# Prompt attention: query tiles in descending order, and the bias strip loaded by head

## What is computed

```python
def attend(q, k, v, bias, mask):
    s = jnp.einsum('bntkgd,bnlkd->bnkgtl', q, k).astype(F32) * HEAD_DIM ** -0.5 + bias
    m = mask[:, None, None]
    p = jax.nn.softmax(jnp.where(m, s, NEG_INF), axis=-1)
    p = jnp.where(m, p, 0.0)
    o = jnp.einsum('bnkgtl,bnlkd->bntkgd', p.astype(v.dtype), v)
    return o, p
...
    g = jax.nn.sigmoid(gate_logit.astype(F32)).reshape(B, T, NSA_KV_HEADS, NSA_GROUP, 3).astype(o_cmp.dtype)
    o = g[..., 0:1] * o_cmp + g[..., 1:2] * o_sel + g[..., 2:3] * o_win
```

## Time and profile before

| what | value |
|---|---|
| median of 3 runs | 1068.53 us (1065.99 to 1071.66) |
| the profiled execution | 1066.85 us |
| its span, first to last instruction | 1064.9 us |
| TensorE busy | 959.9 us, 90% of the span |
| VectorE busy | 450.3 us, 42% |
| ScalarE busy | 310.9 us, 29% |
| GpSimd busy | 268.8 us, 25% |
| mean granted TensorE clock | 0.938 of full speed |

### The profile page before, as it was taken

How to read it: one execution, slowest core, us unless ns; L and a number is a source line. 1 busy time by engine, 2 the same in 40 slices (tenths; PEclk the granted TensorE clock), 3 DMA queues, 4 the chain that set the end, 5 groups by cost and what they waited for, 6 DMA issues and landing times. The chain is left out here.

```text
span 1064.9 us, 21167 instructions
## 1 busy us (share of the span) xinstructions
PE 959.9 (90%) x8113; PEld 632.8 (59%) x8113; DVE 450.3 (42%) x933; ACT 310.9 (29%) x712; POOL 268.8 (25%) x397
## 2 busy tenths in 40 slices
PE   6899999999899989998899998996599999999755
PEld 5456777777666858887455664454455555555422
DVE  2240000003667257785568772437522233333216
ACT  4100000000575213233367642101023232333222
POOL 6000000032102146900256523000223333444110
PEclk9899999999999989999899998997599998899888
DMA  9975642522920030000744252926599999999954
GB/s 309 343 284 215 214 178 100 107 85 75 320 69 7 1 48 3 4 4 7 186 116 119 71 188 107 335 98 256 224 356 381 386 394 380 391 369 366 366 192 146
DMA packets 89227, 207.76 MB, mean 195 GB/s; under 512 B 31526, under 2 KB 54750, under 8 KB 75231
## 3 DMA queue, kind: packets, MB, share of 16 engines
q1 hardware_dynamic: 76226, 182.64, 49.3%
q0 software_dynamic: 10144, 20.47, 6.0%
q10 hardware_dynamic: 2756, 3.27, 0.9%
HBM read 254.83 MB, written 29.75 MB: 267 GB/s over the span
## 5 line engine op out<-in xcount | busy, mean ns | idle before, releaser
L2403 POOL DMA_INDIRECT ys_dram<-late,ids x49 | 45.3, 924 | 155.4 <-ACT late L2605 129.4
L592 PE MATMUL PS<-hT,wring 128*128 128x288 f32 x256 | 83.5, 408 | 0.0
L2787 DVE COPY mixT<-PS 128x128 f32<-128x128 f32 x49 | 14.3, 292 | 163.0 <-PE PS L2513 163.0
L593 PE MATMUL PS<-hT,wring 128*128 128x288 f32 x256 | 83.0, 406 | 0.0
L2397 POOL DMA_INDIRECT mixT<-h_dram,ids x49 | 46.9, 957 | 110.2 <-DVE ids L2754 91.6
L2494 PE MATMUL PS<-ring,mixT 128*64 128x256 f32 x304 | 72.4, 393 | 2.4 <-DVE mixT L2773 2.4
L2495 PE MATMUL PS<-ring,mixT 128*64 128x256 f32 x304 | 72.4, 393 | 0.0
L2494 PEld LDWEIGHTS PS<-ring,mixT 128*64 128x64 f32 x304 | 43.1, 143 | 33.9 <-issue 12.6
L2427 PE MATMUL PS<-late,mixT 128*128 128x512 f32 x128 | 57.7, 611 | 1.8 <-PEq L2854 1.8
L592 PEld LDWEIGHTS PS<-hT,wring 128*128 128x128 f32 x256 | 48.2, 190 | 17.2 <-DVE xc L203 2.6
L593 PEld LDWEIGHTS PS<-hT,wring 128*128 128x128 f32 x256 | 48.6, 190 | 13.4
(11 more groups left out here) (566 smaller groups left out, 2206.0 us busy)
## 6 DMA issues: line engine op xcount, KB each, us to landing
ring<-in_expert_w_gate_dram SPq DMA_DIRECT2D x27, 1024.0 KB
ring<-in_expert_w_up_dram SPq DMA_DIRECT2D x27, 1024.0 KB
ring<-in_expert_w_down_dram SPq DMA_DIRECT2D x27, 1024.0 KB
late<-in_w_ada_dram SPq DMA_DIRECT2D x8, 2048.0 KB
mod_r<-in_expert_w_gate_dram SPq DMA_DIRECT2D x9, 1024.0 KB
mod_r<-in_expert_w_up_dram SPq DMA_DIRECT2D x9, 1024.0 KB
mod_r<-in_expert_w_down_dram SPq DMA_DIRECT2D x9, 1024.0 KB
late<-in_expert_w_gate_dram SPq DMA_DIRECT2D x7, 1024.0 KB
```

Source lines behind the costliest of these rows:

```text
L592: MM(PS[:, b, 0:HALF], lhs, hT[:, k, 0:HALF], **s)
L593: last = MM(PS[:, b + 1, 0:HALF], lhs, hT[:, k, HALF:NTOK], **s)
L2403: pool.indirect_dma_start(m.ys_dram.ap(), bass.IndirectOffsetOnAxis(ap=ids[:, 1, j:j + 1], axis=0), yr(n), None, bounds_check=LAST_ROW, oo ...
```

## The change

Three things are changed together. The prompt's query tiles are taken in descending order, so that the first units have 512 keys and the last 128. The bias strip is loaded by four transfers, one for each g, with the heads g and G + g and all 896 columns, in place of five transfers of all heads and a part of the columns. The waits of VectorE follow: once for each g in the first tile, in place of one for each tile and one for the first compressed unit. `out_of`, which picks the output bank and orders the outputs, counts in the new order.

```diff
-    strip_in = [sem(f"a_strip_in{k}") for k in range(5)]
+    strip_in = [sem(f"a_strip_in{g}") for g in range(G)]
...
-    for i in range(PT):
+    for i in reversed(range(PT)):
         units += [("p", SEL, i, g) for g in range(G)] + [("c", CMP, i, 0)] + [("p", WIN, i, g) for g in range(G)]
...
-    out_of = lambda u: units[u][2] + (PT if units[u][0] == "s" else 0)
+    out_of = lambda u: PT + units[u][2] if units[u][0] == "s" else PT - 1 - units[u][2]
...
-            for k, (lo, hi) in enumerate(((SEQ - P, SEQ), (SEQ, STRIP), (SEQ - 2 * P, SEQ - P), (P, 2 * P), (0, P))):
-                sp.dma_start(strip[:, :, lo:hi], bass.AP(m.rb_rep, RB_C - (SEQ - P) + lo, [[H * RB_W - 1, P], [RB_W, H], [1, hi - lo]])).then_inc(strip_in[k], 16)
+            for g in range(G):
+                sp.dma_start(strip[:, g::G, :], bass.AP(m.rb_rep, g * RB_W + RB_C - (SEQ - P), [[H * RB_W - 1, P], [G * RB_W, KV], [1, STRIP]])).then_inc(strip_in[g], 16)
...
                 if kind == "p":
-                    if br == SEL and g == 0:
-                        dve.wait_ge(strip_in[a if a == 0 else a + 1], 16)
+                    if br == SEL and a == PT - 1:
+                        dve.wait_ge(strip_in[g], 16)
...
                 elif kind == "c":
-                    if a == 0:
-                        dve.wait_ge(strip_in[1], 16)
...
                 if kind == "p":
-                    if a == 0 and g == 0:
+                    if a == PT - 1 and g == 0:
                         pe.wait_ge(pt_v if br == SEL else pt_a, 1)
```

## The result

Over 20 runs of each, the changed kernel has a median of 1071.88 us (1066.88 to 1076.64), the kernel before 1068.22 us (1060.23 to 1072.42): ratio 1.0037, 95% interval 1.0019 to 1.0055. The forecast was 1072 us, 0.3% above the 1068.53 us of the runs shown then.

What follows compares the result with a forecast made beforehand. Attention is paced in turn by a VectorE-ScalarE loop and by TensorE. Loads 1.1, order 3.6, sample head minus 2.4 and front clock 1.7 sum to plus 4.0 us: 1072 forecast, range 1065 to 1079.

Steps and rivals of the forecast that it cites:

- Start: First attention unit waits for 0.393 MB more of the bias strip: plus 1.1 us.
- The later strips: Bias loads after the first come 2.5 us apart, units want them at least 2.87 apart: hidden, no cost.
- Width changes: Prompt tiles in descending order, wide turning and values beside narrower scores: 90.3 against 86.75 us, plus 3.6.
- Tile 3: First prompt tile now: four units at 2.87, five at 3.11, 27.0 us against 24.6 without outputs and key copies, plus 2.4.
- Tile 0: Last prompt tile now: 15.92 less 3.0 of low clock, plus 1.72, 2.6 and 0.5, giving 17.7 us.
- The kernel before at full clock: Front of attention, tile 0 in the old order: the low clock loses 3.0 us.
- Head of the samples: First sample group after the prompt tiles falls from 10.71 to 8.3 us with one-block units left over: minus 2.4.
- Clock at the front: Start of attention: clock falls again, somewhat later, for 3.4 us at half rate, a lag of 1.7 us.
- Rival 1: Clock stays low at the front ten us or more under 512-key units: 5 in place of 1.7, 1076; chance 0.18.
- Rival 2: Clock falls under tile 0 at the prompt's end, the 3.0 us only change place: 1075.5; chance 0.10.
- Rival 3: Wide turns and values behind narrower scores are absorbed, tiles 2 and 1 lose their 3.7: 1069; chance 0.20.
- Rival 4: Strips land together, first unit waits for 3.67 MB, some 7 us go: 1079; chance 0.07.

Runs made afterwards that it cites:

- the second pair of profiles: The changed kernel and the kernel before, each profiled again with no code change; attention 143.00 us and 139.52 us.
- thinner values: Changed kernel with added front matmuls, two of four key blocks left out of tile 3's window value products; tile 2 22.82 us in place of 25.41.
- the order alone: Kernel before with query tiles descending, strip still loaded by columns; attention 151.26 us, total ratio 1.0127 (1.0058 to 1.0196).

## Why the prediction was right

The total, 1072, the sign and the size of attention's part (plus 4.0 forecast; plus 3.7 and, from the second pair of profiles, 3.5 measured) came out; several terms were off and made up for one another. That the total came out to 0.1 us is luck: the same code against itself was 0.5% off.

- Start: 1.1 forecast, 0.7 measured (4.74 against 4.06); the second pair's 0.6 is not the strip's, as both waited for TensorE. The queue moved 430 GB/s in the microsecond from 521, more than either rate I had. The Trainium skill, page "DMA: Bandwidth & Descriptors", section Specifications, puts the HBM limit of a core near 358 GB/s and asks for no more than 512 B a transfer for line rate. Here runs of 512 and 1,536 bytes went at 290 to 372 GB/s and runs of 3,584 bytes at 398 to 430 in the microseconds from 519 to 526, so the measurement decides for this case. The Trainium skill, page "Perfetto Trace Analysis", section Roofline, allows a core that works alone some 435 GB/s, and with that the trace agrees. The later strips were hidden, as forecast.
- Width changes. At full clock tiles 3, 2, 1, 0 take 25.74, 25.40, 20.66, 18.41 (forecast 27.0, 25.0, 20.6, 17.7), 90.22 together (90.3). Tile 2 and 1 were right to 0.4 and 0.1, and the cause, backlog on TensorE, was shown for tile 2 by thinner values. Tile 3 was over-priced by 1.3: its first four units took 11.0 us (11.5 forecast) and the five behind 14.7 (15.6), as only three of these stand 3.1 us apart; the step behind the compressed unit is 2.58 and the last 2.87. Tile 0 was under-priced by 0.7, and the next term explains it: from 13.80 us, the kernel before at full clock, the forecast's own additions (1.72, 2.6 and 0.5) give 18.6, 0.2 above the 18.41 measured. The key copies cost 2.7 there, so their price was right, TensorE's wait of 2.38 us at step 34 included.
- The kernel before at full clock: I took 3.0 us off tile 0, the run with added matmuls took off 2.1. The 3.0 came from the spacing of two units (1.97 against 1.43) for the whole low stretch.
- Head of the samples: minus 2.4 forecast, minus 3.7 measured, and 0.4 more in the second group, which I hadn't priced.
- Clock at the front: a fall was forecast between 526 and 530 and came at 529.7; it lasted 6.8 us in place of 3.4, cost 2.3 in place of 1.7, and showed as the idle of 2.27 us at the first window unit. Rival 1, ten us or more, came true in the second profile for the length (10.2 us), not the price: tile 3 took 28.32, 2.6 more than at full clock, where I had 5. In the first profile TensorE's second turning waits 1.53 us for a copy of ScalarE, in this one not at all, so part of the slow work filled waits that were there anyway. In the order alone 13.2 us of low clock under tile 3, from its start on, cost 1.3 (27.05). The place of the stretch counts for more than its length.
- Rival 2, a fall under tile 0, I had set beside the forecast; it came together with the front's, in most profiles, and costs 1.5 us (19.97 and 19.92 against 18.41).
- Rival 3 fell: nothing was absorbed, in any order. Rival 4 fell with the first score operation at 4.74 us; the order alone, which waits for all four pieces, stands at 13.70.

The account, at full clock: the order adds 5.7 us to the prompt (90.22 against 84.56) and takes 3.7 and 0.4 from the samples: plus 1.5. The clock costs the changed kernel 2.3 and 1.5, the one before 2.1: plus 1.7. The loads: plus 0.7. Sum 3.9, measured 3.7; the stage's last part, behind the start of the last sample group, was 0.15 shorter.

## What to carry to other kernels

In a software pipeline whose later steps work on earlier, wider units, a falling order makes narrow steps pay for wide ones where the engine of the later steps is near the limit, and gives part of it back behind the loop; here 5.7 us against 4.1. A rising order does the reverse. Choose loads to fit the order: what the first unit needs whole must come first, and the next pieces at the pace of the units. And compare stage by stage in traces when total times scatter more than the change is worth.

## What the runs showed of the hardware that was not expected

The clock's fall under the same instructions is not fixed: 6.8 us in one profile of the changed kernel and 10.2 in the other; 10.2 in one profile of the kernel before, 6.8 and a later 3.4 in the other. The Trainium skill, page "TensorE: Matmul & The Clock Gate", Part 1, calls the cold matmuls of one kernel "run-variable"; the traces agree: tile 1 of the kernel before took 18.88 and 20.16 us. The scores of two heads, 64 rows each on different halves of the rows, take as long as those of one (0.92 and 0.91 us). And the same queue carried 3,584-byte runs at up to 430 GB/s, where 512-byte runs had gone at 290.
